# Packing the small parameters and the narrow projection columns into two blocks laid out by the host

## The chip, the cores and the metric

The kernel runs on one core of a Trainium2 chip. The metric is the device time of one execution in microseconds (us). The median of three runs is 2736.48 us (2736.41 to 2740.3).

## What is computed

Four transformer layers over one sequence of 256 tokens with model width 1024, all in float32. Two layers of a first kind: RMS norm, a projection `h @ w_in` that feeds four branches (forgetting attention, gated linear attention, retention with rotary tables, and a state-space branch with a causal convolution of width 4) and four gates, an up-projection of each branch, a gated sum, `w_out`; then RMS norm and a SwiGLU of width 2816. Two layers of a second kind with other branches, the first with a SwiGLU, the last with a mixture of eight experts of width 3584, two per token.

```python
u = h @ w_in                                   # 1024 x 8220, with narrow parts ff (4), glr (16), dt (8)
y_a = forgetting_attention(heads(fq), heads(fk), heads(fv), ff + fox_bf, fox_qn, fox_kn)
log_a = log_sigmoid(glr @ gla_w2 + gla_b) / GLA_TAU
xbc = silu(causal_depthwise_conv(xbc, conv_w, conv_b)); dt = softplus(dt + dt_bias)
merged = g0*(y_a @ w_up_a) + g1*(y_b @ w_up_b) + g2*(y_c @ w_up_c) + g3*(y_d @ w_up_d)
x = x + merged @ w_out
```

Each layer brings small parameters: norm gains, convolution taps and biases, per-head constants, the lambda vectors of the last kind of attention, and the token positions.

## The kernel before, in words

**Weights.** Every large matrix is streamed as chunks of 128 x 2048 floats (1 MB). A chunk is loaded by two DMAs of 512 KB on the queue of SyncE (SP) into one of RAW = 6 slots (`columns`, L470, L471; L474 for a run in two pieces). ScalarE (ACT) rounds it to `w_hi` (L1127, one of HI = 3 slots), VectorE (DVE) writes the remainder over the raw data as `w_lo` (L1521). TensorE (PE) multiplies each chunk three times: hi by hi, hi by lo, lo by hi (L600 to L602). The semaphores are `raw_full` (DMA to ACT), `hi_ready` (ACT to DVE), `lo_ready` (DVE to PE) and `w_used` (PE back to SP and ACT). SP may load chunk 6 only when chunk 0 is used, and so on: from there on the stream is paced by PE.

**The start.** SP issues `x` (two DMAs), chunks 0 to 5, then the function `parameters` with 23 small DMAs of gains, taps and lambdas (L504), and then waits for `w_used`. ACT issues the identity, the first gains (`cols1[:, l, 0:8]`, two DMAs, L1448), runs one Exp, and then issues the three narrow column groups of `w_in` for both layers (`wsm`, L1451), two bias rows, `gla_w2`, and the constants `cst` (796 KB, L1467). GpSimd (POOL) issues `onehot`, `tab`, `glab`, the positions, two head vectors and four DMAs of query and key gains (L2157). PE transposes `x` into the four banks X[0] to X[3] (L589); ACT evicts each with its gain into `xhi` (two per bank, after waiting for `gain1_loaded`), DVE writes `xlo` (L1531). ACT's program is in order: it does its first eviction only after all its DMA issues.

```python
for i in range(4):                 # ACT, norm(); DVE's lo_tiles() follows it
    ... xhi of bank X[i]
if n == 0:
    conv(0)
    conv(1)
statistics()                       # squares of x, Ln, Exp (before wsm_hi)
```

**The first mixer.** PE waits for X[0] and X[1], multiplies chunk 0, waits for X[2], X[3] and `cst_loaded`, then does the narrow product (L682 to L684), for which DVE must have written `wsm_lo` (L1558), which waits for ACT's `wsm_hi`, which comes after `statistics()`. Then chunk 1, a small matmul for the bias rows, and so on. At position 1 DVE runs `setup()` (L2070), which waits for `cst` and for all the small parameters of SP and POOL.

Of the kernel before, what the change touches and what calls it, by code (L numbers as in the profile page):

```python
# [9 lines left out]
I32 = mybir.dt.int32  # L10
# [20 lines left out]
RAW = 6  # L31
# [8 lines left out]
W1SMALL = [(1540, 16), (768, 4), (4116, 8)]  # L40
# [82 lines left out]
def program(nc, a, out, stop=99):  # L123

    ctx = ExitStack()
    with ctx:
# [26 lines left out]
        g_at = top[0]  # L153
# [17 lines left out]
        cst = sb("cst", [P, NC])  # L171
# [5 lines left out]
        ident_t = sb("ident_t", [P, P])  # L177
        cols1 = sb("cols1", [P, L1, 60])
        cols2 = sb("cols2", [P, L1, 25])
        heads8 = sb("heads8", [P, L1, 16])  # L180
        lam_in = sb("lam_in", [P, L1, 4, 32])
        lam = sb("lam", [P, L1, 6])
        small = sb("small", [P, 64])
        epst = sb("epst", [P, 2])
        conv2 = sb("conv2", [P, L1, 6])
        nstat = sb("nstat", [P, 8])
        type1_at = top[0]
        brow = sb("brow", [P, L1, 12])
# [27 lines left out]
        router = sb("router", [P, KT, NE])  # L216
# [18 lines left out]
        ang = sb("ang", [P, 4, NT, 32], at=g_at + 24576)  # L235
        posi = sb("posi", [P, NT], I32, at=g_at + 25600)
        posf = sb("posf", [P, NT], at=g_at + 25600 + 64)
# [28 lines left out]
        def sem(name):  # L266
            return ctx.enter_context(nc.semaphore(name))
# [8 lines left out]
        x_loaded, cst_loaded, par_loaded = sem("x_loaded"), sem("cst_loaded"), sem("par_loaded")  # L276
        par_sp_loaded = sem("par_sp_loaded")
# [4 lines left out]
        gain1_loaded, narrow_loaded, tiles_set = sem("gain1_loaded"), sem("narrow_loaded"), sem("constant_tiles_set")  # L282
        setup_v, setup_s = sem("setup_vector"), sem("setup_scalar")
# [172 lines left out]
        def _(sp):  # L456
# [45 lines left out]

            def load(dst, src):
                sp.dma_start(dst, src).then_inc(par_sp_loaded, 16)  # L504

            def by_tile(name, dst, taps=False):

                for l in range(L1):
                    load(dst[:, l], a[name][l].rearrange("w (k p) -> p (w k)" if taps else "(k p) -> p k", p=P))

            def parameters():
                for name, cc in (("gla_norm", 18), ("ret_norm", 20)):
                    for h in range(2):
                        load(cols1[64 * h:64 * h + 64, :, cc], a[name].rearrange("l p -> p l"))
                by_tile("ln2", cols1[:, :, 8:16])
                by_tile("ssd_norm", cols1[:, :, 22:26])
                by_tile("ssd_conv_w", cols1[:, :, 28:52], True)
                by_tile("ssd_conv_b", cols1[:, :, 52:58])
                by_tile("mix_norm_g_2", cols2[:, :, 0:8])
                by_tile("ffn_norm_g_2", cols2[:, :, 8:16])  # L520
                by_tile("conv_w_2", conv2[:, :, :], True)
                by_tile("pool_scale_2", cols2[:, :, 21:23])
                for h in range(2):
                    load(cols2[64 * h:64 * h + 64, :, 23], a["diff_subln_g_2"].rearrange("l p -> p l"))
                load(lam_in[:, :, :, :], a["diff_lambda_2"].partition_broadcast(P))

            for t in range(NT):
                sp.dma_start(x[:, t, :], a["x"][0, t * P:t * P + P, :]).then_inc(x_loaded, 16)
            for k in phases:
# [3 lines left out]
                if k[0] in ("mix1", "mix2"):  # L533
# [3 lines left out]
                    for n, run in enumerate(runs):  # L537
                        if c0 == RAW:

                            parameters()  # L540
                        columns(c0, w, 0, run)
                        columns(c0 + 1, w, 4, run)
                        c0 += 2
# [573 lines left out]
        def _(act):  # L1117
# [25 lines left out]
            def norm(k, n, ready, before=lambda t: None):  # L1143
# [22 lines left out]
                if n == 0:  # L1166
                    act.wait_ge(gain1_loaded, 16 * L1)
                for i in range(4):
# [277 lines left out]

            def gain(dst, src):
                act.dma_start(dst, src).then_inc(gain1_loaded, 16)  # L1448

            def narrow(dst, src):  # L1450
                act.dma_start(dst, src).then_inc(narrow_loaded, 16)  # L1451

            act.dma_start(ident_t[:, :], a["ident"]).then_inc(ident_loaded, 16)
            for l in range(L1):
# [12 lines left out]
            act.dma_start(cst[:, :], a["cst"]).then_inc(cst_loaded, 16)  # L1467
            n = 0
# [37 lines left out]
        def _(dve):  # L1506
# [28 lines left out]
            def norm(k, n):  # L1535
                l, f = k[1], k[2]
                if n == 0:
                    dve.wait_ge(gain1_loaded, 16 * L1)
                if f is None:
# [11 lines left out]
                for i in range(4):  # L1551
                    lo_tiles(X[i], norm_hi, 4 * n + i + 1, i, col)
                if n == 0:
                    conv(0)
                    conv(1)
                if f == "mix1":
# [588 lines left out]
        def _(pool):  # L2145
            G = nc.gpsimd
            links = [0]
            loads = [0, 0]

# [12 lines left out]
            pool.dma_start(glab[:, :], a["gla_b"][0].partition_broadcast(P)).then_inc(glab_loaded, 16)  # L2162
            load(posi[:, :], a["positions"][0].rearrange("(t p) -> p t", p=P))
            load(heads8[:, :, 0:8], a["ssd_a_log"].partition_broadcast(P))
            load(heads8[:, :, 8:16], a["ssd_d"].partition_broadcast(P))

            for name, cc in (("fox_qn", 26), ("fox_kn", 27)):
                for h in range(2):
                    load(cols1[64 * h:64 * h + 64, :, cc], a[name].rearrange("l p -> p l"))
            assert loads[0] == NPAR_POOL, loads  # L2170

            def build(k, h, col, slot):
# [66 lines left out]
            for k, ready in zip(phases, XREADY):  # L2239
                if k[0] == "norm" and k[2] == "mix2" and k[1] == 0:  # L2240
# [5 lines left out]
                    for l in range(L1):  # L2246
                        load(wgrp[:, l], a["pool_w_2"][l].rearrange("g c d -> c g d"), True)
                    load(router[:, :, :], a["moe_router_2"][0].rearrange("(k p) n -> p k n", p=P), True)
                    load(poolw[:, :, :], a["poolw"], True)
                    assert loads[1] == NPAR2, loads  # L2250
                elif k[0] == "norm" and k[2] == "moe":
# [54 lines left out]
```

## Time and profile before

| | |
|---|---|
| median of three runs | 2736.48 us (2736.41 to 2740.3) |
| profiled execution, first to last instruction | 2734.5 us |
| PE busy | 2608.4 us, 95% |
| PE weight load busy | 2151.6 us, 79% |
| DVE busy | 1819.1 us, 67% |
| ACT busy | 1549.9 us, 57% |
| mean granted clock of PE | 0.984 |
| DMA | 623.59 MB, 228 GB/s over the span |

The profile is one execution. No time of its own is listed for it beyond the span; the lowest run is 1.9 us above that span. Starts are counted from the first instruction. A busy PE is not one at its peak: a matmul of 128x512 takes twice as long at half the clock. The expert stage is the last third of the span, where the DMA is busy almost throughout.

### The profile page before, as it was taken

What the parts mean: (1) busy time and instruction counts of PE and PEld (TensorE: products, weight loads), DVE (VectorE), ACT (ScalarE), POOL (GpSimd) and SP (SyncE); (2) the same over time, 40 slices, a digit from 0 to 9 for tenths busy, and PEclk for the clock granted to TensorE, in tenths of its full rate; (3) what the DMA queues carried; (4) which work ended last, traced back from release to release, by engine and by line L of the source; (5) the groups of instructions that cost most, each with busy time, mean ns of one, the idle gap of its engine ahead of it and who ended that gap; (6) DMA issues with size and microseconds to landing.
All of it is one profiled execution on the core that took longest, in us unless ns stands there. A gap on an engine that the chain in (4) does not pass through costs nothing.

```text
span 2734.5 us, 34634 instructions
## 1 busy us (share of the span) xinstructions
PE 2608.4 (95%) x12226; PEld 2151.6 (79%) x12226; DVE 1819.1 (67%) x1749; ACT 1549.9 (57%) x1619; POOL 175.0 (6%) x162
## 2 busy tenths in 40 slices
PE   4899999999999999989999998999999999999997
PEld 3788788788878878878888876878787878787786
DVE  3466754546675554555554466888888888888897
ACT  3544454454445454445445545777777777777776
POOL 1222200022220000020000020000000000000000
PEclk7999999999999999999999998999999999999999
DMA  7344455544445564445554454999999999999996
GB/s 169 126 151 148 154 184 184 171 146 151 150 155 184 184 202 150 154 147 176 185 184 154 139 184 147 351 339 352 337 352 336 355 335 352 323 352 337 343 345 234
DMA packets 452740, 623.59 MB, mean 228 GB/s; under 512 B 46189, under 2 KB 347573, under 8 KB 452656
## 3 DMA queue, kind: packets, MB, share of 16 engines
q1 hardware_dynamic: 442256, 617.89, 67.4%
q0 software_dynamic: 1248, 3.39, 0.5%
q10 hardware_dynamic: 9152, 1.16, 0.3%
q8 instruction: 55, 0.90, 0.1%
q14 instruction: 29, 0.24, 0.0%
HBM read 621.31 MB, written 1.06 MB: 228 GB/s over the span
## 4 chain that ended last, share of the span: by engine, by line
PE 89%; DVE 4%; ACT 3%; issue 2%; ACTq 1%; POOL 1%; DVEq 0%; POOLq 0%
PE bank L600 12%; PE bank L602 12%; PE bank L601 12%; PE bank L1036 7%; PE bank L1038 7%; PE bank L1037 7%; PE bank L615 4%; PE bank L617 4%; PE bank L616 4%; PE bank L1067 4%; PE bank L1069 4%; PE bank L1068 4%; PE bank L589 3%; DVE w_lo L1521 1%; PE bank L1009 1%
## 5 line engine op out<-in xcount | busy, mean ns | idle before, releaser
L1521 DVE TENSOR_TENSOR w_lo<-raw,w_hi 128x2048 fp32r<-128x2048 f32 x587 | 1349.8, 2303 | 550.2 <-ACT w_hi L1127 535.6
L1127 ACT ACTIVATE w_hi<-raw 128x2048 fp32r<-128x2048 f32 x587 | 1122.0, 1915 | 243.8 <-PE bank L617 140.4
L600 PE MATMUL bank<-w_hi,xhi 128*128 128x512 f32 x1456 | 580.2, 398 | 39.9 <-DVE w_lo L1521 34.2
L602 PE MATMUL bank<-w_lo,xhi 128*128 128x512 f32 x1456 | 570.1, 392 | 0.0
L601 PE MATMUL bank<-w_hi,xlo 128*128 128x512 f32 x1456 | 569.2, 391 | 0.0
L1036 PE MATMUL bank<-w_hi,xhi 128*128 128x512 f32 x896 | 359.5, 401 | 9.8 <-DVE w_lo L1521 9.8
L600 PEld LDWEIGHTS bank<-w_hi,xhi 128*128 128x128 f32 x1456 | 275.0, 189 | 96.8 <-issue 39.1
L1038 PE MATMUL bank<-w_lo,xhi 128*128 128x512 f32 x896 | 350.2, 391 | 0.0
L1037 PE MATMUL bank<-w_hi,xlo 128*128 128x512 f32 x896 | 349.6, 390 | 0.0
L602 PEld LDWEIGHTS bank<-w_lo,xhi 128*128 128x128 f32 x1456 | 274.6, 189 | 58.6
L601 PEld LDWEIGHTS bank<-w_hi,xlo 128*128 128x128 f32 x1456 | 275.3, 189 | 54.3
L1127 ACT ACTIVATE ghi<-bank 128x256 fp32r<-128x256 f32 x178 | 64.8, 383 | 249.7 <-PE bank L589 249.7
L1036 PEld LDWEIGHTS bank<-w_hi,xhi 128*128 128x128 f32 x896 | 168.3, 188 | 44.3 <-DVE w_lo L1521 13.2
L1038 PEld LDWEIGHTS bank<-w_lo,xhi 128*128 128x128 f32 x896 | 168.2, 188 | 35.5
L1037 PEld LDWEIGHTS bank<-w_hi,xlo 128*128 128x128 f32 x896 | 168.7, 188 | 31.4
L1067 PE MATMUL bank<-w_hi,ghi 128*128 128x512 f32 x448 | 175.1, 391 | 12.8 <-DVE glo L1993 12.8
L1068 PE MATMUL bank<-w_hi,glo 128*128 128x512 f32 x448 | 174.3, 389 | 0.0
L1069 PE MATMUL bank<-w_lo,ghi 128*128 128x512 f32 x448 | 174.3, 389 | 0.0
L615 PE MATMUL bank<-w_hi,xhi 128*128 128x512 f32 x272 | 110.3, 405 | 5.7 <-DVE xlo L1531 5.7
L1067 PEld LDWEIGHTS bank<-w_hi,ghi 128*128 128x128 f32 x448 | 84.1, 188 | 32.6 <-issue 14.7
L616 PE MATMUL bank<-w_hi,xlo 128*128 128x512 f32 x272 | 108.9, 400 | 0.0
L617 PE MATMUL bank<-w_lo,xhi 128*128 128x512 f32 x272 | 108.7, 400 | 0.0
(333 smaller groups left out, 2636.1 us busy)
## 6 DMA issues: line engine op xcount, KB each, us to landing
raw<-in_moe_w SPq DMA_DIRECT2D x676, 512.0 KB, 5.1
raw<-in_w_in SPq DMA_DIRECT2D x232, 512.0 KB, 4.6
raw<-in_w_ffn_in SPq DMA_DIRECT2D x88, 512.0 KB, 4.6
raw<-in_dense_w SPq DMA_DIRECT2D x66, 512.0 KB, 4.1
raw<-in_w_ffn_out SPq DMA_DIRECT2D x44, 512.0 KB, 3.7
raw<-in_w_out SPq DMA_DIRECT2D x32, 512.0 KB, 3.9
raw<-in_branch_proj SPq DMA_DIRECT2D x16, 512.0 KB, 3.7
raw<-in_w_up_d SPq DMA_DIRECT2D x8, 512.0 KB, 3.6
```

The source lines that it names most:

```text
L600: mm(bank[banks[t]][:, :], xhi[:, k0 + k, tok], wh, start=start and k == 0, stop=False)
L601: mm(bank[banks[t]][:, :], xlo[:, k0 + k, tok], wh, start=False, stop=False)
L602: last = mm(bank[banks[t]][:, :], xhi[:, k0 + k, tok], wl, start=False, stop=stop and k == 3)
L615: mm(b, xh, hi[:, h, o:o + 512], start=first and k == 0, stop=False)
L1036: mm(bank[b][:, :], xhi[:, kt, 0:P], hi[:, h, w], start=kt == 0, stop=False)
L1037: mm(bank[b][:, :], xlo[:, kt, 0:P], hi[:, h, w], start=False, stop=False)
L1038: last = mm(bank[b][:, :], xhi[:, kt, 0:P], lo[:, s, w], start=False, stop=kt == KT - 1)
L1067: mm(o, ghi[:, m, 0, :], hi[:, h, w], start=first, stop=False)
L1068: mm(o, glo[:, m, 0, :], hi[:, h, w], start=False, stop=False)
L1069: last = mm(o, ghi[:, m, 0, :], lo[:, s, w], start=False, stop=final)
L1127: return nc.scalar.activation(dst, src, f, **kw)
L1521: V.tensor_tensor(lo[:, c % RAW, :], raw[:, c % RAW, :], hi[:, c % HI, :].bitcast(F32), ALU.subtract).then_inc(lo_ready, 1)
```

## The change

The host builds two arrays. `par` (128 x 512 floats, 2 KB per partition) holds all small parameters already in the layout of SBUF, with the constant columns that DVE's memsets wrote before, the broadcast rows repeated for every partition, and the positions as raw bits. `narrow` (128 x 448 floats) holds the narrow columns of `w_in` for both layers. ACT loads each with one DMA, right behind the identity, then `gla_w2`, before the wait for `tiles_set` and the Exp. The old single loads are gone: the two of L1448 and five of L1451 on ACT, 23 on SP, seven on POOL. `cst` moves from the end of ACT's list to SP, behind chunks 0 and 1 and ahead of chunk 2. On ACT and on DVE `conv(0)` moves between banks X[1] and X[2] of the first norm; `conv(1)` stays behind X[3]. `setup()` waits for `cst` alone. PE's program is untouched.

```diff
@@ tiles
+        par = sb("par", [P, NPARF])
+        def group(name, n):
+            return par[:, PAR[name][0]:PAR[name][0] + n]
...
@@ SP
-            def parameters():
...
                     for n, run in enumerate(runs):
-                        if c0 == RAW:
-                            parameters()
+                        if c0 == 2:
+                            sp.dma_start(cst[:, :], a["cst"]).then_inc(cst_loaded, 16)
                         columns(c0, w, 0, run)
@@ ACT, norm (DVE's norm alike)
                 if n == 0:
-                    act.wait_ge(gain1_loaded, 16 * L1)
+                    act.wait_ge(par_loaded, 16)
                 for i in range(4):
...
                     last.then_inc(norm_hi, 1)
-                if n == 0:
-                    conv(0)
-                    conv(1)
+                    if n == 0 and i % 2 == 1:
+                        conv(i // 2)
                 statistics()
@@ ACT, start
             act.dma_start(ident_t[:, :], a["ident"]).then_inc(ident_loaded, 16)
-            for l in range(L1):
-                gain(cols1[:, l, 0:8], a["ln1"][l].rearrange("(k p) -> p k", p=P))
+            act.dma_start(par[:, :], a["par"]).then_inc(par_loaded, 16)
+            act.dma_start(wsm[:, :, :, :].rearrange("p l k n -> p (l k n)"), a["narrow"]).then_inc(narrow_loaded, 16)
+            act.dma_start(gw2[0:16, :, :], a["gla_w2"].rearrange("l r n -> r l n")).then_inc(narrow_loaded, 16)
             act.wait_ge(tiles_set, 1)
             link(go(nstat[:, 0:1], epst[:, 0:1], ACT.Exp))
-            o = 0
-            for f, w in W1SMALL:
-                narrow(wsm[:, :, :, o:o + w].rearrange("p l k n -> p (l k) n"),
-                       a["w_in"].rearrange("l (k p) n -> p (l k) n", p=P)[:, :, f:f + w])
-                o += w
-            narrow(brow[:, :, 0:4], a["fox_bf"].partition_broadcast(P))
-            narrow(brow[:, :, 4:12], a["ssd_dt_bias"].partition_broadcast(P))
-            narrow(gw2[0:16, :, :], a["gla_w2"].rearrange("l r n -> r l n"))
-            act.dma_start(cst[:, :], a["cst"]).then_inc(cst_loaded, 16)
@@ DVE
-                dve.wait_ge(par_loaded, 16 * NPAR_POOL)
-                dve.wait_ge(par_sp_loaded, 16 * NPAR_SP)
...
-            V.memset(epst[:, 1:2], 1e-5)
-            V.memset(cols1[:, :, 16:18], 1.0)
-            V.memset(cols2[:, :, 17:21], 1.0).then_inc(tiles_set, 1)
+            V.memset(epst[:, 1:2], 1e-5).then_inc(tiles_set, 1)
@@ POOL
-            load(posi[:, :], a["positions"][0].rearrange("(t p) -> p t", p=P))
-            load(heads8[:, :, 0:8], a["ssd_a_log"].partition_broadcast(P))
-            load(heads8[:, :, 8:16], a["ssd_d"].partition_broadcast(P))
-            for name, cc in (("fox_qn", 26), ("fox_kn", 27)):
-                for h in range(2):
-                    load(cols1[64 * h:64 * h + 64, :, cc], a[name].rearrange("l p -> p l"))
```

## Rows read from the trace of the kernel before

**Rows 1.** The page: span, and busy time of the engines.
```profile
span 2734.5 us, 34634 instructions
PE 2608.4 (95%) x12226; PEld 2151.6 (79%) x12226; DVE 1819.1 (67%) x1749; ACT 1549.9 (57%) x1619; POOL 175.0 (6%) x162
```

**Rows 2.** Waits of the first 60 us: who waited for whom, total, times, longest.
```profile
PE bank L600 <- DVE w_lo L1521: 31.6, 1, 31.6
ACT xhi L1127 <- issue: 30.1, 1, 30.1
```

**Rows 3.** Timeline of the start: start us, us, engine line op, count, [idle before].
```profile
2.27 1.28 ACT L1127 ACT_TABLE_LOAD   x1 [2.27 <-issue]
...
3.79 24.15 ACTq L1451 DMA_DIRECT2D wsm<-in_w_in  x3
...
6.27 3.35 PE L589 MATMUL bank<-ident_t,x 128*128 128x128 f32 x16 [6.27 <-DMA x<-in_x]
...
33.87 3.02 ACT L1127 ACTIVATE xhi<-bank,cols 128x256 fp32r<-128x256 f32 x8 [30.11 <-issue]
...
36.73 3.76 ACT L1127 ACTIVATE w_hi<-raw 128x2048 fp32r<-128x2048 f32 x2
...
38.73 4.50 DVE L1521 TENSOR_TENSOR w_lo<-raw,w_hi 128x2048 fp32r<-128x2048 f32 x2 [0.65 <-ACT w_hi L1127]
...
41.16 0.77 PE L600 MATMUL bank<-w_hi,xhi 128*128 128x512 f32 x1 [31.55 <-DVE w_lo L1521]
...
49.61 0.43 SPq L470 DMA_DIRECT2D raw<-in_w_in  x1
```

**Rows 4.** DMAs issued at 1.1, 2.1 and 32.9 us: KB each, us to landing.
```profile
x<-in_x SPq DMA_DIRECT2D x1, 512.0 KB, 5.0
...
raw<-in_w_in SPq DMA_DIRECT2D x1, 512.0 KB, 11.2
...
cst<-in_cst ACTq DMA_DIRECT2D x1, 796.0 KB, 9.3
```

**Rows 5.** Stretches: start:end, length, busy PE, PEld, DVE, ACT, POOL, PEclk, DMA, GB/s.
```profile
0.00:5.00 5.00, 0.00 (x0) 0.00 (x0) 0.38 (x12) 1.49 (x2) 3.94 (x11) 1.00 0.65 195
4.00:5.00 1.00, 0.00 (x0) 0.00 (x0) 0.00 (x0) 0.00 (x0) 1.00 (x3) 1.00 1.05 412
8.00:9.00 1.00, 1.00 (x6) 1.00 (x6) 0.00 (x0) 0.00 (x0) 0.11 (x1) 1.00 1.71 149
9.00:10.00 1.00, 0.61 (x5) 0.38 (x3) 0.00 (x0) 0.00 (x0) 0.00 (x0) 1.00 0.64 36
12.00:13.00 1.00, 0.00 (x0) 0.00 (x0) 0.00 (x0) 0.00 (x0) 0.00 (x0) 0.80 1.13 340
46.00:47.00 1.00, 1.00 (x4) 0.85 (x3) 0.39 (x1) 1.00 (x2) 0.00 (x0) 0.64 0.68 5
```

**Rows 6.** DMA queues from 8 to 9 us: packets, MB, share (q0 POOL, q1 SP).
```profile
q0 software_dynamic: 40, 0.01, 124.6%
q1 hardware_dynamic: 78, 0.14, 41.8%
```

**Rows 7.** Timeline from 40 us: from the statistics to the narrow product.
```profile
40.34 1.10 ACT L1127 ACTIVATE hrow<-x 128x1024 f32<-128x1024 f32 x1
...
45.96 0.39 ACT L1127 ACTIVATE wsm_hi<-wsm 128x224 fp32r<-128x224 f32 x1
...
46.25 1.90 ACT L1127 ACTIVATE w_hi<-raw 128x2048 fp32r<-128x2048 f32 x1
46.38 0.39 DVE L1558 TENSOR_TENSOR wsm_lo<-wsm,wsm_hi 128x224 fp32r<-128x224 f32 x1 [3.16 <-ACT wsm_hi L1127]
...
49.30 0.28 PE L682 MATMUL bank<-xhi,wsm_hi 128*28 128x256 f32 x1
```

**Rows 8.** Waits of PE from 41.2 us to the end.
```profile
PE bank L589 <- DVE u L1904: 15.3, 4, 5.5
```

**Rows 9.** The expert stage as one stretch, columns as in rows 5.
```profile
1740.00:2680.00 940.00, 919.72 (x4200) 748.55 (x4200) 810.24 (x599) 677.98 (x555) 0.00 (x0) 1.00 1.00 343
```

More of the change, by code:

```diff
@@ L100, with parameter_block, cols, twice @@
 constants()
+PAR = {}
+def parameter_block(v):
+    def cols(m):
+        return m.reshape(L1, -1, P).transpose(2, 0, 1)
+    def twice(m):
+        return np.concatenate([m, m], 1).T[:, :, None]
+    def same(m):
+        return np.broadcast_to(m[None], (P,) + m.shape)
+    one = lambda n: np.ones((P, L1, n), np.float32)
+    none = lambda n: np.zeros((P, L1, n), np.float32)
+    taps = lambda m: np.concatenate([cols(m[:, w]) for w in range(m.shape[1])], 2)
+    half = lambda m: np.concatenate([twice(m), none(1)], 2)
+    parts = [
+        ("cols1", [cols(v["ln1"]), cols(v["ln2"]), one(2), half(v["gla_norm"]), half(v["ret_norm"]), cols(v["ssd_norm"]),
+                   twice(v["fox_qn"]), twice(v["fox_kn"]), taps(v["ssd_conv_w"]), cols(v["ssd_conv_b"]), none(2)]),
+        ("cols2", [cols(v["mix_norm_g_2"]), cols(v["ffn_norm_g_2"]), none(1), one(4), cols(v["pool_scale_2"]), half(v["diff_subln_g_2"])]),
+        ("heads8", [same(v["ssd_a_log"]), same(v["ssd_d"])]),
+        ("conv2", [taps(v["conv_w_2"])]),
+        ("brow", [same(v["fox_bf"]), same(v["ssd_dt_bias"])]),
+        ("lam_in", [same(v["diff_lambda_2"].reshape(L1, P))]),
+        ("posi", [v["positions"][0].reshape(NT, P).T.copy().view(np.float32)]),
+    ]
+    at, out = 0, []
+    for name, ms in parts:
+        m = np.concatenate(ms, ms[0].ndim - 1).reshape(P, -1)
+        m = np.concatenate([m, np.zeros((P, -m.shape[1] % 8), m.dtype)], 1)
+        PAR[name] = (at, m.shape[1])
+        at += m.shape[1]
+        out.append(m)
+    return np.ascontiguousarray(np.concatenate(out, 1).astype(np.float32))
+def narrow_block(v):
+    w = np.concatenate([v["w_in"][:, :, f:f + n] for f, n in W1SMALL], 2)
+    return np.ascontiguousarray(w.reshape(L1, KT, P, 28).transpose(2, 0, 1, 3).reshape(P, L1 * KT * 28))
+NPARF = sum(n + -n % 8 for n in (L1 * 60, L1 * 25, L1 * 16, L1 * 6, L1 * 12, L1 * 128, NT))
 G1 = {
@@ L177, in program @@
         ident_t = sb("ident_t", [P, P])
[L178 to L181, printed above, removed]
+        par = sb("par", [P, NPARF])
+        def group(name, n):
+            return par[:, PAR[name][0]:PAR[name][0] + n]
+        cols1, cols2, heads8, conv2, brow = (group(name, L1 * n).rearrange("p (l n) -> p l n", l=L1) for name, n in (
+            ("cols1", 60), ("cols2", 25), ("heads8", 16), ("conv2", 6), ("brow", 12)))
+        lam_in = group("lam_in", L1 * P).rearrange("p (l i n) -> p l i n", l=L1, i=4)
+        posi = group("posi", NT).bitcast(I32)
         lam = sb("lam", [P, L1, 6])
@@ L184, in program @@
         epst = sb("epst", [P, 2])
-        conv2 = sb("conv2", [P, L1, 6])
         nstat = sb("nstat", [P, 8])
         type1_at = top[0]
-        brow = sb("brow", [P, L1, 12])
         nar_at = top[0]
@@ L235, in program @@
         ang = sb("ang", [P, 4, NT, 32], at=g_at + 24576)
-        posi = sb("posi", [P, NT], I32, at=g_at + 25600)
         posf = sb("posf", [P, NT], at=g_at + 25600 + 64)
@@ L276, in program @@
         x_loaded, cst_loaded, par_loaded = sem("x_loaded"), sem("cst_loaded"), sem("par_loaded")
-        par_sp_loaded = sem("par_sp_loaded")
         narrow_rounded, narrow_split, glab_loaded = sem("narrow_rounded"), sem("narrow_split"), sem("glab_loaded")
@@ L281, in program @@
             ("par2_loaded", "bias_rows_out", "bias_in", "final_gain_in", "stored"))
-        gain1_loaded, narrow_loaded, tiles_set = sem("gain1_loaded"), sem("narrow_loaded"), sem("constant_tiles_set")
+        narrow_loaded, tiles_set = sem("narrow_loaded"), sem("constant_tiles_set")
         setup_v, setup_s = sem("setup_vector"), sem("setup_scalar")
@@ L501, in feed_forward @@
                      lambda j, it, c: up(j, it, c, 4), down)
-            def load(dst, src):
-                sp.dma_start(dst, src).then_inc(par_sp_loaded, 16)
-            def by_tile(name, dst, taps=False):
-                for l in range(L1):
-                    load(dst[:, l], a[name][l].rearrange("w (k p) -> p (w k)" if taps else "(k p) -> p k", p=P))
-            def parameters():
-                for name, cc in (("gla_norm", 18), ("ret_norm", 20)):
-                    for h in range(2):
-                        load(cols1[64 * h:64 * h + 64, :, cc], a[name].rearrange("l p -> p l"))
[L515 to L525, printed above, removed]
             for t in range(NT):
@@ L1445, in _ @@
             eps1, eps2 = epst[:, 0:1], epst[:, 1:2]
[L1447 to L1451, printed above, removed]
             act.dma_start(ident_t[:, :], a["ident"]).then_inc(ident_loaded, 16)
-            for l in range(L1):
-                gain(cols1[:, l, 0:8], a["ln1"][l].rearrange("(k p) -> p k", p=P))
+            act.dma_start(par[:, :], a["par"]).then_inc(par_loaded, 16)
+            act.dma_start(wsm[:, :, :, :].rearrange("p l k n -> p (l k n)"), a["narrow"]).then_inc(narrow_loaded, 16)
+            act.dma_start(gw2[0:16, :, :], a["gla_w2"].rearrange("l r n -> r l n")).then_inc(narrow_loaded, 16)
             act.wait_ge(tiles_set, 1)
             link(go(nstat[:, 0:1], epst[:, 0:1], ACT.Exp))
-            o = 0
-            for f, w in W1SMALL:
-                narrow(wsm[:, :, :, o:o + w].rearrange("p l k n -> p (l k) n"),
-                       a["w_in"].rearrange("l (k p) n -> p (l k) n", p=P)[:, :, f:f + w])
-                o += w
-            narrow(brow[:, :, 0:4], a["fox_bf"].partition_broadcast(P))
-            narrow(brow[:, :, 4:12], a["ssd_dt_bias"].partition_broadcast(P))
-            narrow(gw2[0:16, :, :], a["gla_w2"].rearrange("l r n -> r l n"))
-            act.dma_start(cst[:, :], a["cst"]).then_inc(cst_loaded, 16)
             n = 0
@@ L1537, in norm @@
                 if n == 0:
-                    dve.wait_ge(gain1_loaded, 16 * L1)
+                    dve.wait_ge(par_loaded, 16)
                 if f is None:
@@ L1552, in norm @@
                     lo_tiles(X[i], norm_hi, 4 * n + i + 1, i, col)
-                if n == 0:
-                    conv(0)
-                    conv(1)
+                    if n == 0 and i % 2 == 1:
+                        conv(i // 2)
                 if f == "mix1":
@@ L2147, in _ @@
             links = [0]
-            loads = [0, 0]
             def link(ins):
@@ L2153, in link, with load @@
                 pool.wait_ge(pool_link, links[0])
-            def load(dst, src, second=False):
-                loads[second] += 1
-                pool.dma_start(dst, src).then_inc(par2_loaded if second else par_loaded, 16)
+            def load(dst, src):
+                pool.dma_start(dst, src).then_inc(par2_loaded, 16)
             pool.dma_start(onehot[:, :], a["onehot"]).then_inc(bias_loaded, 16)
@@ L2162, in _ @@
             pool.dma_start(glab[:, :], a["gla_b"][0].partition_broadcast(P)).then_inc(glab_loaded, 16)
-            load(posi[:, :], a["positions"][0].rearrange("(t p) -> p t", p=P))
-            load(heads8[:, :, 0:8], a["ssd_a_log"].partition_broadcast(P))
-            load(heads8[:, :, 8:16], a["ssd_d"].partition_broadcast(P))
-            for name, cc in (("fox_qn", 26), ("fox_kn", 27)):
-                for h in range(2):
-                    load(cols1[64 * h:64 * h + 64, :, cc], a[name].rearrange("l p -> p l"))
-            assert loads[0] == NPAR_POOL, loads
             def build(k, h, col, slot):
@@ L2246, in _ @@
                     for l in range(L1):
[L2247 to L2250, printed above, removed]
+                        load(wgrp[:, l], a["pool_w_2"][l].rearrange("g c d -> c g d"))
+                    load(router[:, :, :], a["moe_router_2"][0].rearrange("(k p) n -> p k n", p=P))
+                    load(poolw[:, :, :], a["poolw"])
                 elif k[0] == "norm" and k[2] == "moe":
@@ L2279 @@
 TWO_PI_3 = 2 * math.pi - 6.28125 - TWO_PI_2
-NPAR_POOL = 3 + 4
-NPAR_SP = 4 + 8 * L1 + 2 + 1
-NNARROW = 6
+NNARROW = 2
 NPAR2 = L1 + 2
@@ L2290 @@
         "dense_w2_2", "moe_router_2", "moe_w1_2", "moe_w3_2", "moe_w2_2", "final_norm_g_2"]
+_PACKED = ["positions", "ln1", "ln2", "fox_bf", "fox_qn", "fox_kn", "gla_norm", "ret_norm", "ssd_conv_w", "ssd_conv_b", "ssd_dt_bias",
+           "ssd_a_log", "ssd_d", "ssd_norm", "mix_norm_g_2", "conv_w_2", "pool_scale_2", "diff_lambda_2", "diff_subln_g_2"]
 def kernel(**inputs):
@@ L2299 @@
     arrays.update(cst=constants(), ident=identity(), onehot=bias_buckets(), poolw=pool_matrices(), ones8=np.ones((1, 8), np.float32))
+    arrays.update(par=parameter_block(inputs), narrow=narrow_block(inputs))
+    for name in _PACKED:
+        del arrays[name]
     a = {name: nc.dram_tensor(f"in_{name}", v.shape, mybir.dt.from_np(v.dtype), kind="ExternalInput").ap()
```

## The prediction

> **What bounds the kernel now.** I read the page first [rows 1]: PE is busy 95% of the span, DVE 67%, ACT 57%. In the steady state nothing that touches only small parameters can matter, so a gain has to come from the 5% in which PE stands. The list of waits says where [rows 2]: one wait of 31.6 us of PE for the first `w_lo`, and beside it one of 30.1 us of ACT before its first eviction, put down to "issue", that is, to no work that the profile shows. The timeline explains it [rows 3]. PE ends the transposes of `x` at 9.62 us (6.27 + 3.35). ACT is held from 3.79 to 27.9 us by issuing three DMAs of the narrow columns, then issues four more, and evicts first at 33.87. Then follow 8 evictions (3.02 us), the rounding of chunk 0 (from 36.73), its remainder on DVE (from 38.73) and the first matmul at 41.16. Nearly all of the 31.6 us is thus ACT's queue of issues, not the data: both halves of chunk 0 had landed by 13.3 us (the second issued at 2.09, landing 11.2 later) [rows 4].
>
> The clock is the second reading [rows 5]: granted 0.80 in the stretch from 12 to 13 us, so it fell at 12.6, 3.0 us after PE's last transpose, and 0.64 from 46 to 47, so it rose at 46.7, some 5.5 us after the first matmul. Chunk 0 runs mostly at 1.2 GHz: 8.1 us from 41.16 to the narrow product at 49.30 [rows 3, 7].
>
> **ACT's part.** Removed from its queue before the first eviction: 24.15 us of narrow issues, then the four DMAs up to 33.8 us [rows 3]. Added: two issues like the one on SP that took 0.43 us [rows 3]; with the identity and `gla_w2` ACT has issued all by about 2.9 us, and with the table load that started at 2.27 us before (1.28 us) [rows 3] and the Exp, which was over by 3.79, it is ready at about 4.5. From there on the data decide. I choose the bytes as the measure. Ahead of the end of chunk 0 stand, on all queues, `x` 1024 KB, chunk 0 1024, `par` 256, `narrow` 224, `glab` 128, identity 64, `onehot` and `tab` 50, `gla_w2` 32: 2802 KB or 2.87 MB. In the first 5 us the queues moved 0.975 MB (195 GB/s) [rows 5]; the 1.89 MB that remain take 5.6 us at 340 GB/s, and 0.3 us I add for the landing: chunk 0 at 10.9 us. The fast end is 412 GB/s [rows 5], 9.6 us; the slow end is the 13.3 us of before [rows 4]. I stay near the rate of 340 because what broke it before goes away: from 8 to 9 and 9 to 10 us only 149 and 36 GB/s moved [rows 5], while 40 packets of POOL's queue, of 0.01 MB together, took 124.6% of 16 engines' time [rows 6]; POOL's seven small DMAs are among what is removed, and `glab` stays.
>
> `x` shares the engines with 480 KB of the new blocks: up to 1.4 us at 340 GB/s on its landing at 6.1 (1.1 + 5.0) [rows 4]; I take 0.7. PE then transposes from 6.9 to 10.3 us, a bank in 0.84. ACT evicts X[0] and X[1] (1.5 us at 3.02/8 each) by about 9.4, and waits for chunk 0. `par` would have to land after 9.4 to matter; it stands second in ACT's queue.
>
> **The reordering.** From the start of the first rounding to the first matmul passed 4.43 us (36.73 to 41.16) [rows 3]. `conv(0)` now begins when chunk 0 lands, 10.9; the first matmul follows at **15.3 us** instead of 41.16: 25.9 us earlier. Without the move of `conv(0)` X[2] and X[3] would come first; they are evicted in the time in which ACT would wait anyway, so by bytes the move is worth at most some 0.5 us (X[3] is full at 10.3, its eviction ends at 11.1 to 11.5), and it makes these two banks late: ACT 12.8 to 14.3, DVE until 16.9. PE asks for them after chunk 0 only, at 23.4.
>
> **What is late next.** (a) `cst`, 815 KB, now behind chunk 1 on SP: 10.9 + 1.86 MB at 340 = 16.4 us against 23.4: nothing. (b) `wsm_lo`. ACT rounds chunk 1 from 14.3 to 16.2, and from the statistics to the end of `wsm_hi` pass 6.0 us (40.34 to 46.35), DVE needs 0.4 [rows 7]: 22.6 us, against PE's 23.4. This cover is thin: 0.8 us. (c) Chunk 2 lands at about 19.5 us, ACT wants it at 22.1; chunk 3 lands about 3.1 us later and is rounded after the narrow product. SP sends chunk 6 when chunk 0 is used, as before (49.61) [rows 3]; its own list is now short. (d) `setup()` finds all its data. Its instructions stay, two memsets go: nothing. The rest of the waits is between engines (the next longest for PE is DVE's `u` [rows 8]), and moves with the first matmul. Sum: 25.9 us off the start, nothing given back: span 2708.6. The runs' median lies 2.0 us over the span of the profiled execution; I leave that as it is: 2736.5 − 25.9 = **2710.6 us**.
>
> **The clock.** Between the last transpose and the first matmul PE stands 5.0 us, more than the 3.0 after which it fell, so I count chunk 0 at 8.1 us as before. The Trainium skill (page TensorE: Matmul & The Clock Gate, What's actually happening) says that the window over which the hardware judges activity runs freely and is not restarted by the engine. By that the clock may still be at 2.4 GHz here, and chunk 0 would take about 5.5 us. Then PE would reach the narrow product at 20.8 and wait for `wsm_lo` until 22.6: of 2.6 us only 0.8 would be won, 2709.8.
>
> **The rivals.**
> (1) Forecast, chance 0.82: as above, 2710.6. Its own range: first matmul between 14.0 (chunk 0 at 9.6) and 17.7 us (13.3), and later clock falls that come or go with the new phase, which I bound at 4 us to either side: 2705 to 2717.
> (2) The start turns DMA-bound, 0.12. For it: the rate from 8 to 10 us averaged 92 GB/s [rows 5] and the cause of POOL's long packets isn't proven to be in the DMAs removed. If `glab` and the queue from ACT bring the stream down to 137 GB/s for a while, chunk 0 lands late or `cst` takes the place of the old wait: 3.9 MB up to `cst` at 137 end at about 28 to 31 us, PE stands after chunk 0 until then, 5 to 8 us: about 2718. Against it: 340 GB/s in other stretches, on the same queues.
> (3) The time is not passed on, 0.03: a chain other than PE's would be behind the mixer's first part, so that all but 5 us returns: 2731 to 2736. Only data that came from SP's or POOL's early DMAs could do this, and the last of those was issued before 49.61 us [rows 3], when PE had done one chunk. The other case of this kind, that the blocks don't free ACT (an issue of `narrow` that takes as long as before), is in this chance: their rows are whole, 1.8 and 2 KB, against 16 to 64 bytes.
> (4) Slower, 0.03: the expert stage. It takes 940 us with the DMA at a share of 1.00 and 343 GB/s [rows 9]. The change drops 19 input arrays and adds two, so every weight lies at another address. If the stream there ran 2.8% slower (333 GB/s), the 26 us would be gone; at 4%, 2748. Against it: nothing in the rows shows a rate that depends on the array, and PE is busy 919.72 of 940 us, so it is at most partly bound by the stream.
>
> **How the numbers follow.** The predicted time is that of (1). The range of 2703 to 2719 us takes in (1) with its bounds, the kept clock, and most of (2); (3), (4) and some of the tails of the others are outside. A measurement of this kernel can tell about 0.2%, 5.5 us: (1) and (2) are faster by more; (3) is mostly within; (4) is slower. Faster 0.94, same 0.03, slower 0.03.
>
> **What would show it.** Right: ACT's first eviction at 7 to 9 us with PE's bank as releaser; rounding of chunk 0 at about 10.9, released by the DMA; first matmul at 15.3, the long wait of PE at 5 us instead of 31.6; no wait of PE for `cst` and less than 1 us before the narrow product; from there to the end a distance equal to that of before (2734.5 − 41.2 = 2693.3) within 4 us. The bytes are wrong if chunk 0 lands after 12 us; the reordering is wrong if PE waits for X[2], X[3] or `wsm_lo` for more than 1 us. The forecast as a whole is wrong if that distance grows, above all in the expert stage.

## The result and the profile after

| | before | changed |
|---|---|---|
| median | 2736.44 us (2735.82 to 2740.3, 4 runs) | 2710.85 us (2709.74 to 2711.48, 4 runs) |
| ratio | | 0.9903, 95% interval 0.9892 to 0.9915 |
| span of the profiled execution | 2734.5 us | 2707.9 us (its own time 2709.74) |
| mean granted clock | 0.984 | 0.988 |

The change takes 25.6 us off by the medians; 25.9 were forecast. By the spans of the two profiled executions it is 26.6 us (2734.5 less 2707.9). A second timing on another occasion gave 2710.01 us and 0.9902 (0.9886 to 0.9919).

The page of the changed kernel, against [rows 1]:

```profile
span 2707.9 us, 34596 instructions
PE 2606.4 (96%) x12226; PEld 2150.6 (79%) x12226; DVE 1818.4 (67%) x1747; ACT 1550.0 (57%) x1619; POOL 169.9 (6%) x155
```

PE has the same 12226 matmuls and 2 us less busy time. The waits of the first 60 us, against [rows 2]:

```profile
PE bank L622 <- DVE w_lo L1528: 8.5, 2, 5.9
...
ACT xhi L1149 <- PE bank L611: 4.0, 1, 4.0
...
ACT w_hi L1149 <- DMA raw<-in_w_in: 1.9, 1, 1.9
```

PE's long wait fell from 31.6 to 5.9 us. ACT's wait of 30.1 us for "issue" is gone: it waits 4.0 us for PE's first bank and 1.9 us for chunk 0. The timeline, against [rows 3] and [rows 7]:

```profile
1.15 0.45 ACTq L1469 DMA_DIRECT2D par<-in_par  x1
1.63 0.45 ACTq L1470 DMA_DIRECT2D wsm<-in_narrow  x1
2.11 0.81 ACTq L1471 DMA_DIRECT2D gw<-in_gla_w  x1
...
8.40 1.61 ACT L1149 ACTIVATE xhi<-bank,par 128x256 fp32r<-128x256 f32 x4 [3.95 <-PE bank L611]
11.95 1.91 ACT L1149 ACTIVATE w_hi<-raw 128x2048 fp32r<-128x2048 f32 x1 [1.95 <-DMA raw<-in_w_in]
13.76 1.55 ACT L1149 ACTIVATE xhi<-bank,par 128x256 fp32r<-128x256 f32 x4
...
22.57 0.39 ACT L1149 ACTIVATE wsm_hi<-wsm 128x224 fp32r<-128x224 f32 x1
...
7.19 3.27 PE L611 MATMUL bank<-ident_t,x 128*128 128x128 f32 x16 [7.19 <-DMA x<-in_x]
16.33 0.76 PE L622 MATMUL bank<-w_hi,xhi 128*128 128x512 f32 x1 [5.87 <-DVE w_lo L1528]
...
23.00 0.39 DVE L1564 TENSOR_TENSOR wsm_lo<-wsm,wsm_hi 128x224 fp32r<-128x224 f32 x1 [3.05 <-ACT wsm_hi L1149]
...
23.65 0.28 PE L704 MATMUL bank<-xhi,wsm_hi 128*28 128x256 f32 x1
```

The reader is to see three things. The issues of `par` and `narrow` cost 0.45 us each where the three narrow loads held ACT for 24.15 us. Chunk 0's rounding starts at 11.95, released by its DMA. The first matmul follows 4.4 us later, as before (4.43). From the first matmul to the end pass 2691.6 us, against 2693.3. The expert stage is unchanged, against [rows 9]:

```profile
1713.30:2653.30 940.00, 919.74 (x4200) 748.26 (x4199) 809.69 (x598) 677.77 (x555) 0.00 (x0) 1.00 1.00 343
```

One thing was not as expected: the DMA dip from 7 to 9 us is still there. The stretches of the changed kernel (columns as in rows 5), then its queues from 7 to 8 us:

```profile
7.00:8.00 1.00, 0.81 (x4) 0.84 (x5) 0.00 (x0) 0.00 (x0) 0.00 (x0) 1.00 1.33 241
8.00:9.00 1.00, 1.00 (x7) 1.00 (x6) 0.00 (x0) 0.60 (x2) 0.00 (x0) 1.00 0.69 119
9.00:10.00 1.00, 1.00 (x7) 1.00 (x6) 0.62 (x2) 1.00 (x3) 0.00 (x0) 1.00 0.96 358
...
13.00:14.00 1.00, 0.00 (x0) 0.00 (x0) 0.11 (x1) 1.00 (x2) 0.00 (x0) 0.68 1.15 431
...
17.00:18.00 1.00, 1.00 (x4) 0.81 (x3) 1.00 (x3) 1.00 (x3) 0.00 (x0) 0.50 1.10 346
...
20.00:21.00 1.00, 1.00 (x6) 0.84 (x5) 0.00 (x0) 0.97 (x3) 0.00 (x0) 0.91 1.11 349
```
```profile
q0 software_dynamic: 50, 0.08, 84.8%
q1 hardware_dynamic: 38, 0.08, 25.6%
```

It ends a microsecond earlier than before [rows 5], and POOL's queue (q0) again takes most of the engines' time, 84.8%, for 0.08 of the 0.24 MB moved.

### The profile page after: what moved, and what is told of

Its sections match the earlier page's. It is cut to its first block, busy times and chain, and to the rows that moved or that the text cites. A ratio compares the mean times of both kernels' runs of the same rounds, so it can differ in the third digit from the quotient of the medians.

```text
span 2707.9 us, 34596 instructions
## 1 busy us (share of the span) xinstructions
PE 2606.4 (96%) x12226; PEld 2150.6 (79%) x12226; DVE 1818.4 (67%) x1747; ACT 1550.0 (57%) x1619; POOL 169.9 (6%) x155
## 3 DMA queue, kind: packets, MB, share of 16 engines
q0 software_dynamic: 1024, 3.37, 0.5%
## 4 chain that ended last, share of the span: by engine, by line
PE 90%; DVE 4%; ACT 3%; issue 2%; POOL 1%; DMA 0%; ACTq 0%; DVEq 0%; SPq 0%; POOLq 0%
PE bank L622 12%; PE bank L624 12%; PE bank L623 12%; PE bank L1058 7%; PE bank L1060 7%; PE bank L1059 7%; PE bank L637 4%; PE bank L639 4%; PE bank L638 4%; PE bank L1089 4%; PE bank L1091 4%; PE bank L1090 4%; PE bank L611 3%; DVE w_lo L1528 1%; PE bank L1031 1%
## 5 line engine op out<-in xcount | busy, mean ns | idle before, releaser
L622 PE MATMUL bank<-w_hi,xhi 128*128 128x512 f32 x1456 | 579.6, 398 | 14.2 <-DVE w_lo L1528 8.5
L622 PEld LDWEIGHTS bank<-w_hi,xhi 128*128 128x128 f32 x1456 | 274.9, 189 | 70.9 <-issue 13.4
L1089 PEld LDWEIGHTS bank<-w_hi,ghi 128*128 128x128 f32 x448 | 84.1, 188 | 32.7 <-issue 14.7
```

The lines of the kernel that those rows point to most:

```text
L622: mm(bank[banks[t]][:, :], xhi[:, k0 + k, tok], wh, start=start and k == 0, stop=False)
L1089: mm(o, ghi[:, m, 0, :], hi[:, h, w], start=first, stop=False)
```

## The experiments

All edits are against the changed kernel, except the first, which is against the kernel before. The runs were taken on three occasions; the medians of the kernel before on them are 2737.92, 2737.18 and 2736.94 us, and a gain is given against the one of its own occasion. Where a kernel has one time only, that time alone can't show a step of one or two microseconds; the trace can.

### The narrow block alone

```diff
...
-            for f, w in W1SMALL:
-                narrow(wsm[:, :, :, o:o + w].rearrange("p l k n -> p (l k) n"), ...)
+            narrow(wsm[:, :, :, :].rearrange("p l k n -> p (l k n)"), a["narrow"])
```

> The kernel before with the narrow block alone: the three loads of the narrow columns become one, all else stays, the first gains still come by two DMAs of 4-byte elements. Theory (two bounds lie one behind the other, ACT's issues and the landing of what its first eviction needs): ACT has issued all by about 7 us, but the gains land at 18.9 us as before (issued 1.6, landing 17.3 later), so the first eviction starts at about 19, the first matmul 7.3 us later at 26.2, 15 us earlier than before: 2721.5 us, a ratio of 0.9945. Rival (only ACT's blocked queue cost time, the gains would come in time once the narrow pieces are gone): first matmul at 16 to 19 us, 2711 to 2714 us.

Measured: 2727.28 us, ratio 0.9962 (0.9948 to 0.9976), 10.6 us gained. Its timeline:

```profile
3.79 5.53 ACTq L1458 DMA_DIRECT2D wsm<-in_narrow  x1
...
14.40 0.47 ACTq L1470 DMA_DIRECT2D cst<-in_cst  x1
19.32 3.03 ACT L1134 ACTIVATE xhi<-bank,cols 128x256 fp32r<-128x256 f32 x8 [15.56 <-DMA cols<-in_ln]
...
26.62 0.77 PE L607 MATMUL bank<-w_hi,xhi 128*128 128x512 f32 x1 [16.59 <-DVE w_lo L1524]
...
47.62 0.59 SPq L511 DMA_DIRECT2D lam_in<-in_diff_lambda  x1
...
52.45 0.17 DVE L2078 CAST posf<-posi 128x2 f32<-128x2 int32 x1 [5.37 <-DMA lam_in<-in_diff_lambda]
```

The second bound is where the theory put it: ACT has issued all by 14.9 us, yet its first eviction waits until 19.32 for the gains. The first matmul is at 26.62 (26.2 expected, the rival's 16 to 19 falls). The issue of `narrow` takes 5.53 us here, against 0.45 in the changed kernel: the gains' two loads, of 4-byte elements, still stand ahead of it in ACT's queue, and it is issued 2.2 us later. Which of the two makes it longer isn't shown. But only 10.6 of the 14.5 us stay. The last row says where the rest went: SP issues its 23 small loads only behind chunk 5, the last at 47.62, and DVE's `setup()` now waits 5.37 us for it. ACT and PE follow; the waits of PE from 26.7 us to 200 us, and those of the kernel before from 41.2 us to 214:

```profile
PE bank L607 <- DVE w_lo L1524: 24.7, 2, 16.6
```
```profile
PE bank L600 <- DVE w_lo L1521: 34.2, 2, 31.6
```

In each, the second number of us less the last is the second wait: 8.1 us here, 2.6 before, 5.5 more. So the loads on SP, which cost nothing in the kernel before, are a third bound that the earlier start would have met. 14.5 less 5.5 is 9.0, within the interval (6.6 to 14.2 us). Part of the 5.5 comes back soon: if the two traces are compared matmul by matmul, the 200th comes some 10 us earlier than before.

### The parameter block alone

```diff
-            act.dma_start(wsm[...], a["narrow"]).then_inc(narrow_loaded, 16)
...
+            for f, w in W1SMALL:
+                act.dma_start(wsm[:, :, :, o:o + w]..., a["w_in"]...[:, :, f:f + w]).then_inc(narrow_loaded, 16)
...
```

> The changed kernel with the narrow columns loaded as before by three DMAs on ACT, behind the parameter block. Theory (ACT's queue of issues is the first bound): ACT is again held about 24 us, from 1.6 to 26, first eviction at about 27, first matmul about 6 us later at 33, 8 us earlier than before thanks to the shorter tail of the queue and the place of chunk 0's rounding: 2728 us, ratio 0.997. Rival (the narrow issues were slow only because SP's and ACT's small parameters crowded them): the three issues shrink to under 12 us, first matmul before 21, under 2717 us.

Measured: 2730.58 us, ratio 0.9975 (0.9965 to 0.9985), 7.3 us gained against 2728 us forecast.

```profile
1.64 18.17 ACTq L1472 DMA_DIRECT2D wsm<-in_w_in  x3
19.84 8.99 ACTq L1475 DMA_DIRECT2D gw<-in_gla_w  x1
28.86 1.28 ACT L1149 ACT_TABLE_LOAD   x1 [28.86 <-issue]
...
36.23 0.76 PE L622 MATMUL bank<-w_hi,xhi 128*128 128x512 f32 x1 [25.45 <-DVE w_lo L1532]
```

ACT is held again, 27 us including `gla_w2`, whose issue stands behind the pieces and takes 8.99 us instead of 0.81. The first matmul comes 3 us later than I expected for that reason. The rival (the issues shrink under 12 us once the other small loads are gone) falls, though not all of it: the three narrow issues take 18.17 us for the 24.15 of before. The first matmul is 4.9 us earlier than before, and the narrow product (43.44 us) 5.9, as chunk 0 took 7.2 us and not 8.1; the rest of the 7.3 us is within the interval (4.1 to 9.6). Neither block alone gives the whole: 10.6 and 7.3 us against 25.6 together.

### The order of chunk 0 and the banks

The edit is shown for ACT; DVE's is the same.

```diff
-                    if n == 0 and i % 2 == 1:
-                        conv(i // 2)
+                if n == 0:
+                    conv(0)
+                    conv(1)
```

> The changed kernel with conv(0) and conv(1) behind the four banks again, on ACT and on DVE. Theory (chunk 0's landing at 11.9 us is what ends the wait, and ACT would stand from 10.0 until then): X[2] and X[3] are evicted by about 11.6, rounding of chunk 0 starts at 11.95 as in the changed kernel, first matmul at 16.3 within 0.3 us; the reordering gives nothing here; wsm_hi even 0 to 0.6 us earlier. 2710 us within the scatter of one run (2709 to 2712). Rival (the reordering carries a part): the first matmul comes 1.5 us or more later, as two banks' evictions stand ahead of it.

```profile
8.46 3.31 ACT L1149 ACTIVATE xhi<-bank,par 128x256 fp32r<-128x256 f32 x8 [4.10 <-PE bank L611]
11.82 1.91 ACT L1149 ACTIVATE w_hi<-raw 128x2048 fp32r<-128x2048 f32 x1
...
16.20 0.77 PE L622 MATMUL bank<-w_hi,xhi 128*128 128x512 f32 x1 [5.31 <-DVE w_lo L1529]
```

The eight evictions end as chunk 0 lands; the first matmul is at 16.20 against 16.33. The single time was 2713.6 us, above the range expected for it. What was lost, was lost late in the span. From 1600 to 1670 us the clock column of this run shows 0.83, and 0.88 in the profiled execution of the same kernel, timed below:

```profile
1600.00:1670.00 70.00, 56.03 (x255) 45.21 (x254) 42.08 (x95) 27.86 (x41) 19.05 (x12) 0.83 0.35 119
```
```profile
1600.00:1670.00 70.00, 56.14 (x266) 45.83 (x264) 44.42 (x97) 30.23 (x41) 19.83 (x12) 0.88 0.38 124
```

Compared matmul by matmul, the first execution is 1.1 us ahead of the second until the 7400th matmul (at 1602 us), loses 2.4 us up to the 8000th, and another 2.0 in the last 24 us of the span. The traces of the narrow block alone and the parameter block alone have the same two losses (a column of 0.83 from 1627 to 1697 us, where the kernel before has 0.88), and each of these executions is the slowest of its kernel's (2729.71 of five, 2733.27 of nine). So a profiled time can stand some 4 us above the others for this alone. The timed pair:

> The changed kernel itself, timed beside the next one on one chip. Both theories: 2711 us, ratio 0.990 to 0.991.

> The changed kernel with conv(0) behind the four banks, timed. Theory (its single 2713.6 us came from the phase of the clock late in the span, not from the order): the same median as the changed kernel within 1 us, since its first matmul was at 16.20 against 16.33. Rival (the order is worth what the single run showed): 2 to 3 us more than the changed kernel, intervals apart.

Measured on one chip: the changed kernel 2710.01 us (2709.01 to 2710.67), this order 2710.52 us (2710.16 to 2711.98). The ranges overlap: the reordering is worth half a microsecond by the medians and may be worth nothing.

### The constants ahead of chunk 0

```diff
-                        if c0 == 2:
+                        if c0 == 0:
                             sp.dma_start(cst[:, :], a["cst"]).then_inc(cst_loaded, 16)
```

> The changed kernel with the DMA of the constants (796 KB) issued ahead of chunk 0 instead of behind chunk 1. Theory (bytes ahead of the end of chunk 0 set the start): chunk 0 lands 0.815 MB later, at the 340 to 390 GB/s of these stretches 2.1 to 2.4 us: at 14.0 to 14.3 us, first matmul at 18.4 to 18.8, time 2 to 2.5 us longer, about 2713 us. Rival (a fixed latency, the dip from 7 to 9 us or ACT's own queue sets the start): the first matmul stays at 16.3 within 0.5 us, 2710 us.

```profile
14.20 1.91 ACT L1149 ACTIVATE w_hi<-raw 128x2048 fp32r<-128x2048 f32 x1 [4.38 <-DMA raw<-in_w_in]
...
18.58 0.77 PE L622 MATMUL bank<-w_hi,xhi 128*128 128x512 f32 x1 [7.93 <-DVE w_lo L1528]
```

Both rows are where the theory of bytes put them: 0.815 MB more ahead of chunk 0 cost 2.25 us, 362 GB/s. The one time, 2712.44 us, is 1.6 us over the changed kernel's median. The slow stretch stays here too, from 8 to 10 us (176 and 195 GB/s).

### Taking bytes away: `narrow` behind chunk 1, `glab` behind chunk 0

```diff
-            act.dma_start(wsm[...], a["narrow"])...; act.dma_start(gw2[0:16, :, :], ...)...
+                            sp.dma_start(wsm[...], a["narrow"])...; sp.dma_start(gw2[0:16, :, :], ...)...   # c0 == 2
                             sp.dma_start(cst[:, :], a["cst"]).then_inc(cst_loaded, 16)
```

> The changed kernel with narrow and gla_w2 (256 KB) issued by SP behind chunk 1, so that they no longer share the engines with x and chunk 0. Theory (bytes ahead of chunk 0's end): chunk 0 lands 0.26 MB earlier, 0.7 us, at 11.2; first matmul 15.6; wsm_hi is not held up (narrow lands by 16, ACT wants it at 22). Rival (interleaving on the engines costs nothing, or the engines would idle instead): no change, 16.3.

```profile
15.85 0.77 PE L624 MATMUL bank<-w_hi,xhi 128*128 128x512 f32 x1 [5.11 <-DVE w_lo L1528]
```

0.5 us earlier, for 0.7 expected; the one time was 2711.37 us. The narrow product began at 24.08, later than the changed kernel's 23.65, because the clock rose later within chunk 0 in this execution: the matmuls came 0.43 us apart for 5.7 us, and in the changed kernel for 3.8. So this step is right for the first matmul and shows no gain in the time. The slow stretch is still there, with 139 GB/s from 7 to 8 us and 180 from 8 to 9, so `narrow` isn't its cause.

```diff
+            pool.wait_ge(hi_ready, 1)
             pool.dma_start(glab[:, :], a["gla_b"][0].partition_broadcast(P)).then_inc(glab_loaded, 16)
```

> The changed kernel with POOL issuing glab (128 KB, one row repeated for 128 partitions) only when chunk 0 is rounded. Theory (the dip to 241 and 119 GB/s from 7 to 9 us comes with POOL's packets, and what is left of them in the changed kernel is glab): the dip is gone, chunk 0 lands 1.0 to 1.4 us earlier, at 10.5 to 10.9, and the first matmul is at 14.9 to 15.3 instead of 16.3; one run about 2709, within its scatter. Rival (the dip is not glab's): the stretch stays under 250 GB/s and the first matmul at 16.0 or later.

```profile
7.00:8.00 1.00, 0.90 (x5) 0.93 (x6) 0.00 (x0) 0.00 (x0) 0.00 (x0) 1.00 1.07 376
8.00:9.00 1.00, 1.00 (x6) 1.00 (x5) 0.00 (x0) 0.69 (x2) 0.00 (x0) 1.00 1.07 306
```
```profile
15.07 0.77 PE L622 MATMUL bank<-w_hi,xhi 128*128 128x512 f32 x1 [4.33 <-DVE w_lo L1528]
```

The dip is gone and the first matmul comes 1.26 us earlier; one run gave 2708.77 us. So the dip of the changed kernel needs this one load of a row repeated for all partitions. Its 0.13 MB alone would be 0.36 us at 362 GB/s; 0.9 us come on top. But the load is not enough for it. In this run POOL issued it at 12.90 us, its packets ran between 16 and 18 us, and the stream kept its rate:

```profile
16.00:17.00 1.00, 1.00 (x4) 0.75 (x3) 1.00 (x3) 1.00 (x3) 0.00 (x0) 1.00 1.18 378
17.00:18.00 1.00, 1.00 (x4) 0.81 (x3) 1.00 (x1) 0.98 (x3) 0.00 (x0) 1.00 1.01 320
```
```profile
q0 software_dynamic: 48, 0.13, 19.4%
```

The last line is POOL's queue from 16 to 18 us: 19.4% of the engines' time for 0.13 MB. From 7 to 9 us of the changed kernel the same 0.13 MB took 65.6%. What made the packets long there was not tried.

### Chunk 0 in halves, and what is late next

Chunk 0's first DMA gets a semaphore of its own; ACT rounds and DVE subtracts 1024 columns at a time; PE starts its first two k-tiles on the first half.

```diff
...
+                if c == 0:                               # ACT; DVE and PE alike
+                    act.wait_ge(first_in, 16)
+                    go(hi[:, 0, 0:1024], raw[:, 0, 0:1024], ACT.Copy).then_inc(first_hi, 1)
+                    act.wait_ge(raw_full[0], 16)
+                    go(hi[:, 0, 1024:2048], raw[:, 0, 1024:2048], ACT.Copy).then_inc(hi_ready, 1)
+                    return
...
```

> The changed kernel with chunk 0 handed on in two halves from DMA to ACT to DVE to PE (own semaphores for the first half). Theory (the narrow product's wsm_hi, behind the statistics, is the next bound, 0.5 us behind PE now): first matmul at 13.1 instead of 16.3, but the narrow product starts at 23.5 to 23.8 as in the changed kernel, PE waits 2 to 5 us for wsm_lo: nothing gained, 2710 to 2711 us. Rival (the first matmul alone sets everything behind it): 3 us faster, 2707.5.

```profile
13.04 0.47 PE L628 MATMUL bank<-w_hi,xhi 128*128 128x512 f32 x1 [1.98 <-DVE w_lo L1541]
...
22.95 0.38 PE L710 MATMUL bank<-xhi,wsm_hi 128*28 128x256 f32 x1 [4.18 <-DVE wsm_lo L1584]
```

First matmul at 13.04, 3.3 us earlier, and then a new wait of 4.18 us for `wsm_lo`: the thin cover named in the prediction is the next bound. The narrow product starts 0.7 us earlier than in the changed kernel, and this is lost again: the clock column shows 0.50 from 22 to 28 us, after that wait, and ACT's first evacuation of `u` is at 34.05, 2.0 us later than in the changed kernel (32.10). The median, 2708.93 us (2707.0 to 2713.07), lies between theory and rival and does not part them; the wait does. Then `wsm_hi` is moved as well:

```diff
+                    if n == 0 and i == 1:
+                        act.wait_ge(narrow_loaded, 16 * NNARROW)
+                        go(wsm_hi[:, :, :], wsm[:, 0], ACT.Copy).then_inc(narrow_rounded, 1)
                     if n == 0 and i % 2 == 1:
                         conv(i // 2)
...
```

> The same with wsm_hi rounded before chunk 0, in the time in which ACT waits for it, instead of behind the statistics. Theory: now the narrow product follows chunk 0 at once, at 18.8 (full clock throughout) to 21.3 us (half clock first) instead of 23.8, and 2.5 to 5 us stay to the end: about 2707 us, ratio to the kernel before 0.989. Rival (another thing is late at once, chunk 2 or the rows of chunk 1): the narrow product starts early but the evacuation of u stays at 32.1 us, 2710.

Measured: 2706.24 us (2704.67 to 2707.75), ratio 0.9886 (0.9869 to 0.9902). PE doesn't wait for `wsm_lo`; the narrow product starts at 20.46, 3.2 us earlier than in the changed kernel, and the first evacuation of `u` at 28.91 against 32.10. So the 3.2 us stay up to there; at the end of the span 2.2 of them are left between the two profiled executions (2705.7 and 2707.9), while the medians are 4.6 us apart. Last, with the late `glab` too:

> Halves of chunk 0, early wsm_hi, and glab issued after the first rounding, together. Theory: the two gains lie on the same path (landing of chunk 0, then narrow product) and add: chunk 0's halves land about 1.2 us earlier (9.4 and 10.7), first matmul at 12.0 to 12.4, narrow product at 17.5 to 19.5 instead of 20.5; 1 us less than with the halves alone: 2705 us, ratio about 0.988. Rival (wsm_hi, which waits for narrow and gla_w2 at 10.5, now holds the first half): first matmul not before 13 us, no gain over 2706.2.

```profile
12.46 0.77 PE L628 MATMUL bank<-w_hi,xhi 128*128 128x512 f32 x1 [1.80 <-DVE w_lo L1542]
...
19.45 0.28 PE L710 MATMUL bank<-xhi,wsm_hi 128*28 128x256 f32 x1
```

The narrow product is another 1.0 us earlier, at the edge of what was expected, and the profiled span is the shortest of all, 2703.4 us. The median is 2707.05 us (2704.31 to 2709.55), ratio 0.9893 (0.9876 to 0.9909). The last microsecond is seen in the trace and cannot be told in the times. Both versions are 3 to 5 us below the changed kernel by their medians; their intervals against the kernel before overlap with its own.

## Why the prediction was right

- **What bounded the start.** Right: ACT's queue of issues. It was one of three bounds on one path, and only the first was named as such. The narrow block alone showed the other two: the landing of the gains (19.3 us) and SP's late small loads (52.4 us). The prediction had "`setup()` finds all its data. ... nothing", which is true of the whole change, but it did not say that SP's loads would have cost some 5 us had they stayed.
- **Landing of chunk 0.** Forecast 10.9, measured 11.9 (issued 2.09, landing 9.8 later). That is 0.1 us under the 12 us at which the prediction would have called its bytes wrong. Two terms were mis-sized. The first is the rate: from 5 to 11.9 us the stream moved 2.19 MB, 317 GB/s for the 340 forecast. The prediction put the slow stretch of 8 to 10 us on POOL's seven small DMAs and took it away; the late `glab` shows that the dip which remained needed `glab`, 1.26 us. What the seven had added wasn't tried by itself. The second is the bytes: when chunk 0 was complete, 3.20 MB had moved and not the 2.87 of the sum. SP's queue alone had moved 2.43 MB, 0.33 more than `x` and chunk 0 hold, so part of the next loads went ahead of chunk 0's end; at 340 GB/s that is 1.0 us. The late `glab` has these bytes ahead too (SP's queue: 2.46 MB at 10.7 us).
- **`x`.** Forecast landing 6.8 and transposes at 6.9; measured 7.19. Without consequence: ACT still waited 1.95 us for chunk 0.
- **4.43 us from rounding to first matmul.** Measured 4.38. First matmul 16.33 for 15.3.
- **The clock.** Forecast: falls between transposes and matmul, chunk 0 at 8.1 us. It fell (column 0.68 from 13 to 14 us, so at 13.4, 2.9 us after the last transpose) but rose after some 3.8 us at work instead of 5.5, at about 20.2 (0.91 from 20 to 21), and the narrow product came 7.3 us after the first matmul. This gave back 0.8 of the 1.0 us lost on chunk 0's landing. The Trainium skill (page TensorE: Matmul & The Clock Gate, section What's actually happening) says that the window runs freely, so that the moment of the rise depends on where in it the first matmul lands. The traces agree as far as that moment differs between executions of one program: in the second profile of the changed kernel the spacing goes from 0.43 to 0.23 us after some 3.3 us at work, for 3.8 in the first. The clock kept at 2.4 GHz through PE's 5.9 us of standing, which the prediction held possible by that rule, did not come.
- **The thin cover.** 0.8 us forecast between `wsm_lo` and PE; measured 0.26 (23.39 to 23.65). Right as the next bound, shown by the halves.
- **The reordering.** "Worth at most some 0.5 us": 0.5 us by medians whose ranges overlap, 0.1 by the first matmul (16.38 for 16.29).
- **Nothing given back.** The distance to the end was forecast equal within 4 us; it shrank by 1.7, of which 0.8 is chunk 0. Of the rest 0.4 us is there by the 200th matmul (at 69 us); its cause is open.
- **The rivals.** DMA-bound start: the dip was there but cost about 1 us. The slower expert stage did not come: 343 GB/s and 940 us as before.
- **The near-exact total.** It is in part luck. The first matmul came 24.8 us earlier and not 25.9; the clock gave back 0.8 and the later path 0.9, which makes 26.6 by the spans. The medians say 25.6, because the profiled execution is the fastest of its four: the median lies 3.0 us over its span, where the prediction took 2.0. The mechanism is right; the agreement within 0.3 us is closer than its terms were.

## What to carry to other kernels

A load in tiny pieces cost in three places here: in the issuing engine's program (24.15 us of ACT), in its own late landing (the gains, which held the first eviction until 19.3 us once the queue was clear), and in the issue of well-shaped loads behind it in the same queue (8.99 us for `gla_w2`). So ask of each small load which engine issues it, what that engine should be doing then, and who reads it; and after a start has been shortened, look again at the loads that had been free until then. Once the queue is clear, the bytes ahead of the first tile set the start (0.8 MB more cost 2.25 us): put first what the first product needs, and keep the fillers (statistics, roundings of small tiles) out of the path between it and the second.

## What had not been expected of the hardware

- One load of 128 KB whose source is a single row of 1 KB, repeated for 128 partitions and issued by POOL, went with a fall of the whole stream to 241 and 119 GB/s for two microseconds. With it moved away these two stretches ran at 376 and 306. Yet issued ten microseconds later the same load left the stream at 378 and 320. So it is this load in that place, and what in the place does it is open.
- A DMA of 32 KB in large pieces took 8.99 us to issue on ACT where it stood behind three loads in small pieces; behind two loads of whole rows it took 0.81. `narrow`, whole rows too, took 5.53 us behind the gains and 0.45 in the changed kernel. The 256-column loads on SP (L521 in the changed kernel) also take 10.35 us for four.
- The matmuls' spacing and the clock column can disagree at the start. In the second profile of the changed kernel the column says 1.00 from 14 to 17 us, and the matmuls follow each other by 0.43 us, the spacing that the first profile has where its column says 0.50 (17 to 18 us, above):

```profile
14.00:17.00 3.00, 0.71 (x2) 0.64 (x3) 3.00 (x4) 3.00 (x6) 0.00 (x0) 1.00 1.02 382
```
```profile
16.85 0.63 PE L623 MATMUL bank<-w_hi,xlo 128*128 128x512 f32 x1
17.28 0.63 PE L624 MATMUL bank<-w_lo,xhi 128*128 128x512 f32 x1
17.70 0.63 PE L622 MATMUL bank<-w_hi,xhi 128*128 128x512 f32 x1
```

- The idle time alone didn't settle the clock. With the halves PE stood 1.98 us and went on at full spacing (0.23 us); with all three edits it stood 1.80 us and went on at 0.43, until 15.6 us. With the halves and the early `wsm_hi` it stood 2.63 us, went on at 0.23, and at 14.7 us, in the midst of its work, the spacing went to 0.43 until about 18.1 (clock column 0.50 from 15 to 18 us).
